# Stick-breaking masks added to the scores by TensorE, and S5's small sample and final-state operations on GpSimd

## The reference, cut to what matters

```python
def stick_breaking(q, k, v, bias, q_pos, k_pos):
    z = (jnp.einsum('bqhd,bkhd->bhqk', q, k).astype(F32) * (SB_HEAD_DIM ** -0.5)
         + bias.astype(F32)[None, :, None, None])
    valid = k_pos[None, :] < q_pos[:, None]
    log_beta = jax.nn.log_sigmoid(z)
    log_rest = jnp.where(valid, log_beta - z, 0.0)
    tail = lax.cumsum(log_rest, axis=3, reverse=True) - log_rest
    w = jnp.where(valid, jnp.exp(log_beta + tail), 0.0)
    return jnp.einsum('bhqk,bkhd->bqhd', w, v.astype(F32))
```

## Time and profile before

| | |
|---|---|
| median of 3 runs | 674.18 us (674.04 to 674.87) |
| the profiled execution's own time | 674.94 us |
| its span, first to last instruction | 673.1 us |
| mean granted TensorE clock | 1.000 |
| PE busy | 661.4 us |
| DVE, ACT, POOL busy | 569.1, 415.2, 91.2 us |

### The profile page before, as it was taken

The page is one execution under the profiler, slowest core; times in us unless marked ns, Lnnn a source line. Parts: engine busy times, 40 slices in busy tenths (PEclk is TensorE's granted clock), DMA queues, the critical chain, the costliest instruction groups (busy, mean ns, idle before and its releaser), DMA issues. The chain is left out here.

```text
span 673.1 us, 13390 instructions
## 1 busy us (share of the span) xinstructions
PE 661.4 (98%) x5024; PEld 613.4 (91%) x5024; DVE 569.1 (85%) x1195; ACT 415.2 (62%) x690; POOL 91.2 (14%) x90
## 2 busy tenths in 40 slices
PE   8999999999999999999999999999999999999997
PEld 6777887989999999999987787989999999999996
DVE  5999999989998988789588998898999898884653
ACT  5776348758676666655847536786867666663343
POOL 0000010150222222200200000106012222220001
PEclk9999999999999999999999999999999999999999
DMA  8777540746674655664456463354765556555411
GB/s 315 244 274 220 188 130 6 274 112 227 203 255 151 201 187 184 197 192 142 142 179 228 167 206 125 115 200 167 199 211 197 188 170 193 176 196 190 161 57 66
DMA packets 42915, 121.82 MB, mean 181 GB/s; under 512 B 5538, under 2 KB 15170, under 8 KB 42338
## 3 DMA queue, kind: packets, MB, share of 16 engines
q1 hardware_dynamic: 40466, 115.22, 51.7%
q0 software_dynamic: 1088, 4.11, 2.5%
q10 hardware_dynamic: 1296, 1.63, 0.8%
HBM read 115.33 MB, written 5.61 MB: 180 GB/s over the span
## 5 line engine op out<-in xcount | busy, mean ns | idle before, releaser
L1579 DVE TENSOR_TENSOR w_lo<-ring,w_hi 128x1024 fp32r<-128x1024 f32 x144 | 175.4, 1220 | 30.6 <-ACT w_hi L964 29.0
L439 PE MATMUL ps<-x_hi,w_hi 128*128 128x264 f32 x672 | 191.0, 284 | 1.0 <-DVE x_lo L1529 1.0
L440 PE MATMUL ps<-x_lo,w_hi 128*128 128x264 f32 x672 | 190.4, 283 | 0.0
L441 PE MATMUL ps<-x_hi,w_lo 128*128 128x264 f32 x672 | 190.3, 283 | 0.0
L964 ACT CAST w_hi<-ring 128x1024 fp32r<-128x1024 f32 x144 | 150.2, 1043 | 59.4 <-PE ps L441 58.7
L439 PEld LDWEIGHTS ps<-x_hi,w_hi 128*128 128x128 f32 x672 | 126.5, 188 | 1.9 <-issue 1.8
L440 PEld LDWEIGHTS ps<-x_lo,w_hi 128*128 128x128 f32 x672 | 126.6, 188 | 0.0
L441 PEld LDWEIGHTS ps<-x_hi,w_lo 128*128 128x128 f32 x672 | 126.0, 188 | 0.0
L432 PE MATMUL ps<-x,ring 128*128 128x264 f32 x480 | 112.1, 390 | 0.1
L432 PEld LDWEIGHTS ps<-x,ring 128*128 128x128 f32 x480 | 89.1, 190 | 18.9 <-issue 2.2
L439 PE MATMUL ps<-hff_hi,w_hi 128*128 128x264 f32 x352 | 100.0, 284 | 0.0
(11 more groups left out here) (364 smaller groups left out, 1091.0 us busy)
## 6 DMA issues: line engine op xcount, KB each, us to landing
ring<-in_units SPq DMA_DIRECT2D x187, 512.0 KB, 3.5
kv<-in_kpool SPq DMA_DIRECT2D x32, 128.0 KB, 2.4
kv<-in_vpool SPq DMA_DIRECT2D x32, 128.0 KB, 2.4
SR<-in_sret SPq DMA_DIRECT2D x2, 1024.0 KB, 5.9
out_rsample<-SR POOLq DMA_DIRECT2D x2, 1024.0 KB, 5.1
out_kv<-hb ACTq DMA_DIRECT2D x2, 528.0 KB, 4.4
VBC<-v_rows POOLq DMA_DIRECT2D x8, 128.0 KB, 3.5
out_y<-x SPq DMA_DIRECT2D x3, 264.0 KB, 2.1
```

The costliest lines, as they stand in the source:

```text
L439: mm(out, wh, hi, start=start, stop=False)
L440: mm(out, wh, lo, start=False, stop=False)
L441: return mm(out, wl, hi, start=False, stop=stop)
L1579: E.did(tt(w_lo[:, slot], ring[:, ring_slot(L * UNITS + i)], w_hi[:, slot].bitcast(F32), ALU.subtract), "w_lo")
```

## The change

1. `causal` no longer closes the two score products of a head by themselves. A third matmul adds to the diagonal blocks a tile that is 0 where the key is seen and -2^30 where it isn't: float32r, identity (128 x 128) as weights, 2 x 128 columns. Its two inputs `ident_r` and `unseen_r` are cast once by ACT, in layer 0 at `sc`, and PE's `sb_scores` waits for both. The constant 0/1 tile in `cst` is replaced by this one.
2. DVE's four multiplications by the mask per layer go. PE's products with the weights wait for ACT's exponential (`wexp`) instead of `w`.
3. `s5_states`, `s5_samples` and `s5_finals` go word for word from DVE to POOL. They count under the semaphore `samples`. POOL runs both halves one after another at the head of a layer, and in layer 0 ahead of `v_rows_back`. New waits: POOL for `cf` and `buev`; ACT, before it copies the second half's input products, for the first half's samples; PE, within `s5_c` before the sample products, for the half's samples; SP, for the next layer's parameters, in place of `dve_x0`.

```diff
@@ causal
-                mm(bank[:, 0:SEQ], kk[:, 0:P], qq[:, 0:SEQ], start=True, stop=True)
-                return mm(bank[:, SEQ:DEC], kk[:, P:SEQ], qq[:, P:SEQ], start=True, stop=True)
+                mm(bank[:, 0:SEQ], kk[:, 0:P], qq[:, 0:SEQ], start=True, stop=False)
+                mm(bank[:, SEQ:DEC], kk[:, P:SEQ], qq[:, P:SEQ], start=False, stop=False)
+                diagonal = bank.rearrange("p (a c) -> p a c", a=2)[:, :, 0:P]
+                return mm(diagonal, ident_r[:], bcast(unseen_r[:], [P, 2, P], 1), start=False, stop=True)
@@ sb_scores
                 needr(pe, "rawh", 2 * L, RAW)
+                pe.wait_ge(S("unseen"), 2)
@@ s5_c
+                pe.wait_ge(S("samples"), samples_done(L, hf))
                 for c in range(2):
                     for jj in range(HJ):
@@ sb_values, sb_sample_values
-                need(pe, "w", L, 1)
+                need(pe, "wexp", L, 1)
@@ s5_evac
                 if hf == 1 and c == 0:
                     need(act, "s5rd", L, 1)
+                    act.wait_ge(S("samples"), samples_done(L, 0))
@@ act, tile loop
                     if i == at_["sc"]:
+                        if L == 0:
+                            act.wait_ge(S("ld_cst"), 16)
+                            E.did(nc.scalar.copy(ident_r[:], C["ident"]), "unseen")
+                            E.did(nc.scalar.copy(unseen_r[:], C["unseen"]), "unseen")
                         need(act, "zst", L, 1)
@@ dve
-                E.did(stt(SPL[:], Z[:], 0.0, SPL[:], ALU.max, ALU.add))
-                E.settle()
-                d0, d1 = diagonals(SPL)
-                E.did(tt(d0, d0, mask, ALU.mult))
-                E.did(tt(d1, d1, mask, ALU.mult), "spl")
+                E.did(stt(SPL[:], Z[:], 0.0, SPL[:], ALU.max, ALU.add), "spl")
...
-            def sb_mask(L):
-                need(dve, "wexp", L, 1)
-                d0, d1 = diagonals(Z)
-                E.did(tt(d0, d0, mask, ALU.mult))
-                E.did(tt(d1, d1, mask, ALU.mult), "w")
@@ pool
+            def s5_states(L, hf):
+                if hf == 0:
+                    pool.wait_ge(S("ld_x0"), 16 * (L + 1))
+                    need(pool, "cf", L, 1)
...
             for L in range(DEPTH):
+                for hf in range(2):
+                    s5_states(L, hf)
+                    E.settle()
+                    s5_samples(L, hf)
+                    E.settle()
                 if L == 0:
                     v_rows_back(L)
+                s5_finals(L)
                 need(pool, "s5st", L, 1)
@@ constants
-                    np.ones((P, P), f), (k < q).astype(f), np.full((P, P), 1 / 256, f),
+                    np.ones((P, P), f), np.where(k < q, 0, UNSEEN).astype(f), np.full((P, P), 1 / 256, f),
```

More of the change, by code:

```diff
@@ L95 @@
 N_VEC = 2 * KT + DEPTH * PER_LAYER
-CONSTS = ["mean_v", "mean_d", "ident", "tri", "ones", "mask", "mean_w", "less_mean"]
+CONSTS = ["mean_v", "mean_d", "ident", "tri", "ones", "unseen", "mean_w", "less_mean"]
 LOG_GAMMA = np.log1p(-np.exp2(-5.0 - np.arange(HEADS)))
@@ L104 @@
 ROUND = 1.5 * 2.0**23
+SAMPLE_HALF = 6 + 8
+SAMPLE_STEPS = 2 * SAMPLE_HALF + 5
+UNSEEN = -2.0**30
 ROUND_15 = 1.5 * 2.0**8
@@ L293, in hybrid_step, with samples_done @@
                 "xe": len(X_DVE), "xo": KT - len(X_DVE), "used": UNITS}
+        def samples_done(L, hf):
+            return L * SAMPLE_STEPS + SAMPLE_HALF * (hf + 1)
         def split_count(L, i):
@@ L339, in layer_params @@
                     need(sp, "bu", L - 1, 4)
-                    sp.wait_ge(S("dve_x0"), L * 2)
+                    sp.wait_ge(S("samples"), samples_done(L - 1, 1))
                     sp.dma_start(s5in[:], A["s5in"][L]).then_inc(S("ld_s5in"), 16)
@@ L1747, in s5_pre @@
                     E.did(nc.vector.tensor_tensor_scan(BI[:, jj, tm], m, P3[:, jj, tm], 0.0, ALU.mult, ALU.add))
[L1749 to L1775, removed]
             def s5_post(L, hf):
@@ L2154, in _ @@
         def _(pool):
-            E = Engine(pool, "pool_step")
+            E = Engine(pool, "samples")
             tt = nc.gpsimd.tensor_tensor
@@ L2164, in ln_squares, with s5_samples, s5_finals @@
                           "lnacc2" if t == KT - 2 else "pool_ln")
+            def s5_states(L, hf):
+                if hf == 0:
+                    pool.wait_ge(S("ld_x0"), 16 * (L + 1))
+                    need(pool, "cf", L, 1)
+                jr = slice(hf * HJ, (hf + 1) * HJ)
+                ar, ai = bcast(are[:, jr], [P, HJ, NS], 2), bcast(aim[:, jr], [P, HJ, NS], 2)
+                x0r, x0i = s5x0[:, 0, jr], s5x0[:, 1, jr]
+                E.did(tt(stmp[:, 0], ar, x0r, ALU.mult))
+                E.did(tt(stmp[:, 1], ai, x0i, ALU.mult))
+                E.did(tt(stmp[:, 2], ar, x0i, ALU.mult))
+                E.did(tt(stmp[:, 3], ai, x0r, ALU.mult))
+                E.settle()
+                E.did(tt(stmp[:, 0], stmp[:, 0], stmp[:, 1], ALU.subtract))
+                E.did(tt(stmp[:, 2], stmp[:, 2], stmp[:, 3], ALU.add))
+            def s5_samples(L, hf):
+                jr = slice(hf * HJ, (hf + 1) * HJ)
+                fr, fi = (bcast(v[:, jr], [P, HJ, NS], 2) for v in (fre, fim))
+                need(pool, "buev", L, 2 * hf + 2)
+                br, bi = BR[:, :, SEQ:T], BI[:, :, SEQ:T]
+                if L > 0 and hf == 0:
+                    pool.wait_ge(S("st_s5"), 16 * L)
+                E.did(tt(smul[:, 0], fr, br, ALU.mult))
+                E.did(tt(smul[:, 1], fi, bi, ALU.mult))
+                E.did(tt(smul[:, 2], fr, bi, ALU.mult))
+                E.did(tt(smul[:, 3], fi, br, ALU.mult))
+                E.settle()
+                E.did(tt(smul[:, 0], smul[:, 0], smul[:, 1], ALU.subtract))
+                E.did(tt(smul[:, 2], smul[:, 2], smul[:, 3], ALU.add))
+                E.settle()
+                E.did(tt(s5o[:, 0, jr, 1:NS + 1], stmp[:, 0], smul[:, 0], ALU.add))
+                E.did(tt(s5o[:, 1, jr, 1:NS + 1], stmp[:, 2], smul[:, 2], ALU.add))
+            def s5_finals(L):
+                need(pool, "s5x", L, 2)
+                E.did(tt(lmul[:, 0], fre[:], sfin[:, 0], ALU.mult))
+                E.did(tt(lmul[:, 1], fim[:], sfin[:, 1], ALU.mult))
+                E.did(tt(lmul[:, 2], fre[:], sfin[:, 1], ALU.mult))
+                E.did(tt(lmul[:, 3], fim[:], sfin[:, 0], ALU.mult))
+                E.settle()
+                E.did(tt(s5o[:, 0, :, 0], lmul[:, 0], lmul[:, 1], ALU.subtract))
+                E.did(tt(s5o[:, 1, :, 0], lmul[:, 2], lmul[:, 3], ALU.add), "s5st")
             def v_rows_back(L):
```

32 lines of the change are left out of this document (6 added, 26 removed).

## The result

| | before | after |
|---|---|---|
| median | 674.30 us (674.04 to 674.87, 4 runs) | 683.77 us (682.55, 683.43, 684.11, 685.50) |
| ratio, 95% interval | | 1.0141 (1.0118 to 1.0165) |
| the profiled execution, and its span | 674.94, 673.1 us | 682.55, 680.8 us |
| mean granted clock of TensorE | 1.000 | 0.994 in the profiled one; 0.995, 0.991 and 0.991 in the others |

A forecast was written before the change was run, and what follows sets the result against it. PE, busy 98% of the span, was taken to bound the kernel; +2.6 us in layer 0 and +1.1 in layer 1 gave +3.7 on 674.18, so 677.9 us, own range 676.3 to 679.1, wider range 675.6 to 680.2.

The forecast's parts named there:

- forecast 1.01: Layer 0, before S5's first output products: PE's waits of 0.28 us for ACT and 0.73 for DVE both go.
- The 0.24 us at 109.92: Layer 0: PE's wait of 0.24 us there goes, because DVE is 0.6 us sooner without the finals.
- the further gain of 0.3 at the low parts of x: Layer 0: DVE's earlier finals also take part of PE's 0.5 us wait there, 0.3 taken between 0 and 0.5.
- 675.6 to 680.2: Forecast's wider range in us, said to leave out rivals 1 and 3 and most of 2.
- the sum's own bounds: Range 676.3 to 679.1 us, from the bounds on four heads, the casts and the gain at the LayerNorm.
- Per head I take 0.95: Scores on PE, both layers: each head takes 0.95 us (bounds 0.77 and 1.05), four heads 3.8 against 1.61.
- zero cost to PE: Layer 0, first half's fourteen S5 operations on GpSimd: 0.3 us each, so PE never waits for them.
- rival 2: GpSimd too late for layer 0's first output products: 682 us at 1.14 us an operation, 690 at 1.7; chance 0.10.
- my threshold of 0.84: Layer 0: PE waits for GpSimd's fourteen first-half operations only if one takes over 0.84 us.
- Rivals 1: Scores: heads still run together despite the masks, only 4 x 0.12 us a layer added: 675.1 us; chance 0.09.
- 3: DVE's relief pays at PE's waits, 3.7 us including LayerNorms, with masks at 1.0 us: 673.4 us; chance 0.05.
- 4: Layer 0 scores: products could be done before ACT's casts matter; excluded by the order, no size or chance given.

The follow-up runs named there:

- run 1: Changed kernel with ACT's two casts made three evacuations earlier, so PE has no wait before layer 0's scores: 679.06 us, ratio 1.0068.
- run 6: Changed kernel with small S5 operations back on DVE, casts early, and the four mask matmuls behind all heads' products: 674.09 us, ratio 0.9997.
- run 7: Changed kernel with S5 operations back on DVE, casts early, each mask matmul on its head's 64 rows only (half the mask sum omitted): 674.35 us.
- run 9: Changed kernel with small S5 operations back on DVE and casts early, order still product, product, 128-row mask per head: 679.96 us, ratio 1.0074.
- run 5: Changed kernel with small S5 operations back on DVE; mask matmuls, late casts and PE's wait kept: 684.9 us, ratio 1.0143.
- run 2: Changed kernel with four extra matmuls on constants keeping PE busy during layer 0's wait for the casts: median 682.60 us, ratio 1.0110.
- run 4: Changed kernel without mask matmul, casts and their wait; masks multiplied on DVE as before, small S5 operations on GpSimd: 678.57 us, ratio 1.0064.
- run 10: Changed kernel with S5 operations back on DVE and mask matmuls grouped behind all products, casts left late: 675.53 us, ratio 1.0023.

## Why the prediction was wrong

- **The direction and its first cause: right.** TensorE pays in full for what it is given, VectorE's 10.8 us less buy only the waits listed. The pairs broke up as described, the wait came where and as long as said (1.98 us idle, 2.05 counted from the turn; forecast 1.95), ended by the second cast at 46.3, and 1.1 us were absorbed at S5's output products (forecast 1.01). The 0.24 us at 109.92 came as forecast, the further gain of 0.3 at the low parts of x did not (1.0 us before and after).
- **The step that failed: the clock.** The sum priced every instruction on TensorE at the clock of the rows before, 1.00, and had no term for a fall of it. In the series of heads the granted clock fell to 0.5 for some 7 us in the profiled run: 3.0 us, and up to 6 in others. Runs 1, 6, 7 and 9 show that the series is enough for it, without the wait, and that a mask as such is not; with the casts late it falls sooner and costs more (runs 5 and 9), and why is open. It is this term alone that leaves the range: at full clock about 679.6 us was worked out, and 679.61 measured for nearly the same program (run 2), inside 675.6 to 680.2. It is not inside the sum's own bounds, 676.3 to 679.1 (which should read 676.0 to 679.2 if its parts are simply added); that is the next point.
- **Mis-sized: "Per head I take 0.95".** It is 1.16 us, above my upper bound of 1.05. I took a change of rows to cost 0.2 us for entry and exit from one place, the 32-row products in the earlier trace rows, where it is paid once for eight passes, and added at most 0.28 us a head for both changes and gaps. What a head takes above 0.65 + 0.12 is 0.39 us, and grouped masks start 0.14 apart without it (run 6). Four heads are 4.55 us and not 3.8, 1.5 us over both layers.
- **Wrong but hidden: "zero cost to PE" for GpSimd.** I took 0.3 us an operation, "nearer to an eighth of 0.75"; alone it is 0.2, beside DVE 1.2, one per instruction of DVE as rival 2 has it. The first half was done at 64.4 us in the changed kernel. The chain's mean, six slow and eight fast, was (64.4 - 55.2) / 14 = 0.66 and so under my threshold of 0.84; but that threshold stood on a TensorE that is already 3.15 us late, and on the output products, where ACT's copy asks 2.6 us before them (61.54 and 64.17 in the earlier trace rows). By itself this part costs 4.3 us, by way of ACT's copy (run 4): its cover was the lateness that the masks had brought. Rival 2 was a real mechanism, not the one that decided.
- **Rivals 1, 3 and 4** fell: no overlap across the mask on all rows (it does occur with masks on 64 rows, run 7), no gain at the LayerNorms, and the score products wait for `unseen`.

## What to carry to other kernels

Order TensorE's work by how much of the array it uses: a full-array matmul put between row-packed ones ends their overlap and adds the changes of rows, 0.39 us a head here beside its own 0.12 (4.55 us for four heads), where the same matmuls grouped cost 0.14 each (2.18 us). Such a stretch was followed by a clock at half for 3 to 11 us although the busy time shows nothing. Small operations moved to GpSimd are worth it only where nobody waits for them, because each takes as long as the VectorE instruction beside it; follow the chain through the third engine (here ACT) before saying that nobody does. When a change has two parts, time them apart: a part that seems free may be hidden behind the other's loss, and mending one then uncovers it.

## What the runs showed of the hardware that was not expected

The granted clock fell to 0.5 with TensorE busy in every record (runs 1 and 9), held through an idle time of 2 us before grouped products in nine of eleven executions (run 10), and fell behind one of 3.9 us (run 4). In the same program it fell in some executions and not in others, 677.81 to 681.09 us in run 9. Going from 64-row to 128-row matmuls and back adds 0.39 us to a head. An operation of 32 columns on GpSimd takes 0.24 us alone, and 1.2 us beside VectorE's 1.2 us multiplications of two SBUF operands. What exactly in the series brings the clock down stays open, as does why it falls sooner with the casts late, and whether GpSimd's first half would be in time if it could start before `cf`; none of this was tried.
